# Modulation in four quarters on four column tiles, with four projections taken between them

## The reference, cut to what matters

```python
mod = jax.nn.silu(c) @ w_mod[layer] + b_mod[layer]          # 1024 -> 6 * 1024
mod_c = jax.nn.silu(c_ctx) @ w_mod[layer] + b_mod[layer]
sh1, sc1, g1, sh2, sc2, g2 = jnp.split(mod[:, None, :], N_MOD, axis=-1)
h = modulate(rmsnorm(x, norm1_g[layer]), sh1, sc1)           # h * (1 + scale) + shift
hc = modulate(rmsnorm(ctx, norm1_g[layer]), sh1c, sc1c)
k_g_c = heads(hc @ wk_g, GLA_HEADS)
...
(q_na, k_na, v_na, q_g, k_g, v_g, og, z_lr, m_a, m_b) = jnp.split(h @ w_in[layer], IN_OFFSETS, axis=-1)
```

## Time and profile before

| what | value |
|---|---|
| median of 3 runs | 3015.01 us (3014.63 to 3015.28) |
| the profiled execution's own time | 3013.45 us |
| its span | 3011.7 us, 33763 instructions |
| mean granted TensorE clock | 0.977 of full speed |
| TensorE matmul busy | 2855.4 us, 95% |
| VectorE, ScalarE, GpSimd busy | 1306.2, 1210.9, 1218.6 us (43%, 40%, 40%) |
| HBM read, written | 267.76 MB, 7.34 MB |

### The profile page before, as it was taken

One profiled execution on the slowest core, in us unless ns is written; L12 is line 12 of the kernel. 1 busy time (PEld: TensorE's weight loads), 2 busy tenths in 40 slices (PEclk: granted clock), 3 DMA queues, 4 the chain that ended last, 5 costly groups with the idle time before them and its releaser, 6 DMA issues.

```text
span 3011.7 us, 33763 instructions
## 1 busy us (share of the span) xinstructions
PE 2855.4 (95%) x13324; PEld 2238.1 (74%) x13324; DVE 1306.2 (43%) x1681; ACT 1210.9 (40%) x1753; POOL 1218.6 (40%) x555
## 2 busy tenths in 40 slices
PE   8997899899999999999998999979999999899997
PEld 4776677688888676677786888867766877778885
DVE  5656432441112667744415202268677353341123
ACT  4346663342223555443334222255545233442222
POOL 1122233344445463343444444436624434444442
PEclk9998999999999999999999999989999999999998
DMA  6333122232222311122231222222101223222221
GB/s 237 102 130 123 65 93 78 98 121 98 98 94 104 105 64 43 59 89 77 77 126 70 98 98 96 100 93 77 63 36 70 91 70 108 88 91 98 91 98 63
DMA packets 88989, 277.29 MB, mean 92 GB/s; under 512 B 10048, under 2 KB 10240, under 8 KB 88832
## 3 DMA queue, kind: packets, MB, share of 16 engines
q1 hardware_dynamic: 88832, 275.14, 25.7%
HBM read 267.76 MB, written 7.34 MB: 91 GB/s over the span
## 4 chain that ended last, share of the span: by engine, by line
PE 79%; DVE 12%; ACT 6%; issue 1%; DMA 1%; POOL 0%; SPq 0%; DVEq 0%; ACTq 0%; POOLq 0%
PE bank L1442 23%; PE bank L1444 23%; PE bank L1443 23%; PE bank L1678 2%; PE bank L1493 2%; PE bank L1628 1%; PE bank L1640 1%; DVE pageF L2395 1%; ACT L1723 1%; DVE pageF L2465 1%; DVE pageF L2469 1%; DVE pageR L2263 1%; PE bank L1669 1%; DVE pageF L1972 1%; DVE pageF L2198 1%
## 5 line engine op out<-in xcount | busy, mean ns | idle before, releaser
L2501 POOL TENSOR_TENSOR wlo<-wraw,whi 128x1024 fp32r<-128x1024 f32 x429 | 1047.4, 2444 | 1499.4 <-ACT whi L1706 1498.7
L1442 PE MATMUL bank<-pageR,whi 128*128 128x512 f32 x3552 | 1446.3, 407 | 65.0 <-ACT pageR L1865 27.4
L1444 PE MATMUL bank<-pageR,wlo 128*128 128x512 f32 x3552 | 1384.5, 390 | 0.0
L1443 PE MATMUL bank<-pageR,whi 128*128 128x512 f32 x3552 | 1384.3, 390 | 0.0
L1442 PEld LDWEIGHTS bank<-pageR,whi 128*128 128x128 f32 x3552 | 675.8, 190 | 247.5 <-issue 98.0
L1443 PEld LDWEIGHTS bank<-pageR,whi 128*128 128x128 f32 x3552 | 676.7, 191 | 153.6 <-issue 25.0
L1444 PEld LDWEIGHTS bank<-pageR,wlo 128*128 128x128 f32 x3552 | 675.1, 190 | 140.5
L1706 ACT ACTIVATE whi<-wraw 128x1024 fp32r<-128x1024 f32 x429 | 450.9, 1053 | 401.6 <-PE bank L1444 392.7
L1746 ACT ACTIVATE pageR<-pageF 128x512 fp32r<-128x512 f32 x136 | 85.9, 632 | 460.5 <-DVE pageF L2257 207.9
L2395 DVE SCALAR_TENSOR_TENSOR pageF<-pageF,prm 128x497 f32<-128x497 f32 (+9 forms) x180 | 202.3, 1124 | 2.7
L1827 ACT ACTIVATE pageF<-bank,smal 128x512 f32<-128x512 f32 x96 | 66.0, 687 | 148.8 <-DVE smal L2163 148.6
(11 more groups left out here) (200 smaller groups left out, 2119.8 us busy)
## 6 DMA issues: line engine op xcount, KB each, us to landing
wraw<-in_wst SPq DMA_DIRECT2D x429, 512.0 KB, 3.5
pageF<-in_wmod SPq DMA_DIRECT2D x96, 256.0 KB, 4.9
pageF<-in_xT SPq DMA_DIRECT2D x16, 256.0 KB, 4.3
pageF<-in_bias SPq DMA_DIRECT2D x16, 256.0 KB, 4.1
kept<-pageF SPq DMA_DIRECT2D x16, 256.0 KB, 4.7
pageF<-kept SPq DMA_DIRECT2D x16, 256.0 KB, 4.2
out_x<-pageF SPq DMA_DIRECT2D x8, 256.0 KB, 2.0
pageF<-in_cT SPq DMA_DIRECT2D x4, 256.0 KB, 9.3
```

What stands on the lines that cost most here:

```text
L1442: e.matmul(o, hi, xh, start=first, stop=False)
L1443: e.matmul(o, hi, xl, start=False, stop=False)
L1444: i = e.matmul(o, lo, xh, start=False, stop=last)
L2501: e.tensor_tensor(wlo[:, b % NH, :, :], wraw[:, b % NR, :, :], bc(whi[:, b % NH, :, :]), ALU.subtract).then_inc(*wlod.up(("wlo", b)))
```

## The change

The modulation's first 2048 columns are laid out in four quarters of 512: quarter q holds the shift and the scale of input tiles 2q and 2q+1, 128 columns each. `mod_mm` multiplies each 128 columns on a column tile of its own, with c padded to 32 stationary columns (c, c_ctx, 30 zeros), so that four results stand below each other in 128 partitions by 128 columns; one copy and one transpose turn a quarter. `planned` writes the steps in another order: the loads begin with c and x, the sum of squares takes every squared x tile in a product of its own (no additions on VectorE, no warm-up), Ln and Exp of x and of the context share their table loads, `h_in` is taken apart in four steps, and four projections (wq_g 0, w_lr, wk_g 0, wv_g 0) run k outermost, with the quarters 1 to 3 and the input tiles they give between their products. Their context parts lie in side banks. `w_next` may put a split every four tiles until it is 3 blocks ahead.

```diff
@@ w_next
-        if s % 8 == 0:
-            self.w_split(s // 8 + NH - 1)
+        if s % 4 == 0 and s >= 16 and self.split < s // 8 + NH:
+            self.w_split(self.split)
@@ planned, loads
-    step("load_fixed", "prm")
-    step("load_fixed", "ccol")
-    step("load_fixed", "cst")
+    step("load_fixed", "ccol")
     for k in range(8):
         pages.take(("X", k))
         step("load_x", k)
...
+        if k == 3:
+            step("load_fixed", "cst")
     for k in range(4):
         pages.take(("XC", k))
         step("load_ctx", k)
+    step("load_fixed", "prm")
+    for q in range(4):
+        if q < 3:
+            p.w_load(q)
         for k in range(8):
-            mod_load(8 * c + k)
+            mod_load(8 * q + k)
@@ planned, start
+    step("first_sums")
...
+    p.w_split(0)
+    step("load_fixed", "wal")
+    step("load_fixed", "tabG")
+    step("first_norms")
+    mod_rows(0)
+    step("first_newton", "x", T)
+    mod_columns(0)
+    h_in(0)
+    step("first_newton", "ctx", TC)
...
+    h_lo(0)
+    hc_in(0)
+    inputs(1)
     p.w_split(1)
+
+    def first_products():
+
+        items = [("wq_g", 0, False), ("w_lr", 0, True), ("wk_g", 0, True), ("wv_g", 0, True)]
+        for name, m, ctx in items:
+            mb.take(("o", name, m))
+            if ctx:
+                sbk.take(("oc", name, m))
+        rows, turned = {(0, 2): 1, (1, 3): 2, (3, 1): 3}, {(1, 0): 1, (2, 1): 2, (3, 3): 3}
+        for k in range(8):
+            for i, (name, m, ctx) in enumerate(items):
+                if (k, i) in rows:
+                    mod_rows(rows[k, i])
+                if (k, i) in turned:
+                    q = turned[k, i]
+                    mod_columns(q)
+                    inputs(2 * q)
+                    inputs(2 * q + 1)
...
+                s = p.w_next((name, m, k))
+                groups = [(("o", name, m), H[k])] + [(("oc", name, m), HC[k])] * ctx
+                step("mm", s, tuple(groups), k == 0, k == 7)
+                yield
@@ main_gla
-        yield from p.wide([("w_lr", 0), ("wk_g", 0)], H, HC)
+        yield from first_products()
@@ tensor
-                    e.matmul(o, csil[:, k, :], F(("wmod", 8 * c + k)), start=k == 0, stop=k == 7).then_inc(
-                        *dot.up(("modm", c, k), ("modb", c)))
+                    x = F(("wmod", 8 * q + k))
+                    w.wait_ge(*when("wmod", 8 * q + k))
+                    for t in range(4):
+                        i = e.matmul(o[32 * t:32 * t + 32, 0:128], csil[:, k, :], x[:, 128 * t:128 * t + 128],
+                                     start=k == 0, stop=k == 7)
+                    i.then_inc(*dot.up(("modm", q, k), ("modb", q)))
+
+            def first_sums():
                 w.wait_ge(*when("cst"))
...
+                for k in range(8):
+                    w.wait_ge(*when("q", "x", k))
+                    i = e.matmul(bank(("qm", "x")), ones, F(("q", "x", k)), start=k == 0, stop=k == 7)
+                i.then_inc(*dot.up(("qm", "x")))
...
+            def mod_columns(q):
+                clear(("modt", q))
                 w.wait_ge(*when("cst"))
...
+                w.wait_ge(*when("modrow", q))
+                e.transpose(bank(("modt", q))[:, 0:128], F(("modrow", q))[:, 0:128], ident).then_inc(
+                    *turn.up(("modt", q)))
@@ scalar
+            def first_norms():
+                norms = (("x", T), ("ctx", TC))
+                w.wait_ge(*when("prm"))
+                for t, width in norms:
+                    clear(("r", t))
+                    w.wait_ge(*when("qm", t))
+                    e.activation(F(("r", t))[:, 0:width], bank(("qm", t))[:, 0:width], ACT.Ln, scale=1.0 / 1024,
+                                 bias=col("eps")).then_inc(*fun.up(("rl", t)))
+                for t, width in norms:
+                    r = F(("r", t))[:, 0:width]
+                    w.wait_ge(*when("rl", t))
+                    e.activation(r, r, ACT.Exp, scale=-0.5).then_inc(*fun.up(("re", t)))
```

More of the change, by code:

```diff
@@ L342, in planned, with mod_rows @@
         step("load_ctx", k)
-    p.w_load(0)
-    for c in (1, 3):
+    step("load_fixed", "prm")
+    for q in range(4):
+        if q < 3:
+            p.w_load(q)
         for k in range(8):
[L346 to L349, removed]
+            mod_load(8 * q + k)
+    sbk.take(("qm", "x"))
+    sbk.take(("qm", "ctx"))
     step("silu_c")
-    sqx, sqc = Squares(p, "x"), Squares(p, "ctx", TC)
     for k in range(8):
[L354 to L358, removed]
-        for k in range(8):
[L360 to L385, removed]
+        pages.take(("q", "x", k))
+        step("x_square", k)
+    step("warm_ln")
+    for k in range(4):
+        pages.take(("q", "ctx", k))
+        step("ctx_square", k)
+    def mod_rows(q):
+        sbk.take(("modb", q))
+        step("mod_mm", q)
+        for k in range(8):
+            pages.give(("wmod", 8 * q + k), ("modm", q, k))
+        pages.take(("modrow", q))
+        step("mod_row", q)
+        sbk.give(("modb", q), ("modrow", q))
+    def mod_columns(q):
+        sbk.take(("modt", q))
+        step("mod_columns", q)
+        pages.give(("modrow", q), ("modt", q))
+        sbk.give(("modt", q), ("A1", q))
     H, HC = [("H", k) for k in range(8)], [("HC", k) for k in range(8)]
     def h_in(k):
-        for name in (("ht", k), ("H", k, "hi"), ("H", k, "lo"), ("hct", k), ("HC", k)):
+        for name in (("ht", k), ("H", k, "hi"), ("H", k, "lo")):
             pages.take(name)
@@ L392, in h_in, with h_lo, hc_in, hc_lo @@
         pages.give(("X", k), ("hs", k), ("q", "x", k))
+    def h_lo(k):
+        step("h_lo", k)
         pages.give(("ht", k), ("H", k, "hi"), ("H", k, "lo"))
+    def hc_in(k):
+        for name in (("hct", k), ("HC", k)):
+            pages.take(name)
+        step("hc_in", k)
+        if k % 2:
+            pages.give(("XC", k // 2), ("hcs", k), ("q", "ctx", k // 2))
+    def hc_lo(k):
+        step("hc_lo", k)
         pages.give(("hct", k), ("HC", k, "hi"), ("HC", k, "lo"))
-    for k in range(4):
+    def inputs(k):
@@ L397, in planned @@
         h_in(k)
-    mod_rows(1)
-    p.w_split(1)
[L400 to L409, removed]
+        hc_lo(k - 1)
+        h_lo(k)
+        hc_in(k)
+    step("first_sums")
+    for t, n in (("x", 8), ("ctx", 4)):
+        for k in range(n):
+            pages.give(("q", t, k), ("qm", t))
+        pages.take(("r", t))
+        pages.take(("rt", t))
@@ L476, in side_gla @@
             yield
+            yield from pause(0)
             for dr in range(2):
@@ L1460, in warm_up @@
-            def warm_up():
-                w.wait_ge(*when("cst"))
-                for i in range(6):
-                    t = e.matmul(bank(("warm",)), ident, cst[:, 0:4, :], start=True, stop=True)
-                t.then_inc(*dot.up(("warm",)))
-            def mod_columns(c, half_, part):
-                o, rw = bank(("modt", c)), F(("modrow", c))
-                clear(("modt", c))
+                    x = F(("wmod", 8 * q + k))
[3 more added lines that the diff above has]
+                                     start=k == 0, stop=k == 7)
@@ L1714, in warm_ln @@
             def warm_ln():
-                e.activation(smal[:, 255:256], col("one"), ACT.Ln).then_inc(*fun.up())
+                w.wait_ge(*when("cst"))
+                e.activation(smal[:, 255:256], ones[:, 0:1], ACT.Ln).then_inc(*fun.up())
             def rstd_act(t, width, scale):
@@ L1941, in scalar @@
             mine = {f.__name__: f for f in (
[L1942 removed]
+                silu_c, w_split, square, warm_ln, rstd_act, x_square, first_norms, mod_row, h_in, hc_in, halves, evict, evict_half, evict_turned, evict_z,
                 to_tokens, gla_gate, gla_gate_ctx, gla_scan, gla_decays, gla_out, soft_exp, na_out, silu_gate, tanh_gate, h2_hi,
```

155 lines of the change are left out of this document (101 added, 54 removed).

## The result

The changed kernel takes 2991.3 us (median of 4 runs, 2989.5 to 2992.8) against 3015.2 for the one before (3014.6 to 3015.8, 4 runs): ratio 0.9921, 95% interval 0.9903 to 0.9938. It is 23.9 us faster. The span of the profiled execution is 2987.7 us against 3011.7.

A forecast was written before the change was run, and what follows sets the result against it. TensorE was taken to bound the kernel, losing the first 49.2 us in which it has no projection to run. A gain of 12.4 us from the profiled 3013.45, with 1.56 added back, gave 3002.6 us, range 2993 to 3014.

The forecast's parts named there:

- Landing, sums, norm, 27.6: Start of the kernel: loads, sums of squares and norm let the first projection start at 27.6 us, not 49.23.
- A quarter's product, 2.9 us: Modulation on TensorE: a quarter's 32 products at 0.085 us each take 2.9 us, between bounds of 1.7 and 6.8.
- Mode changes: Changes of tiling mode around a quarter's block on TensorE: 0.2 us per block.
- Four projections, end 70.8: First four projections, with three quarters, transposes, mode changes and low clock between: done at 70.8 us.
- low clock: TensorE's clock at 0.50 after its idle time from 23.3 to 27.6: taken to cost 2.2 us.
- The wait at 87.71 goes: TensorE's 5.17 us wait in wv_g 1 goes, with 2.4 us of low clock; wv_g 1 ends at 80.7, gain 17.1.
- What is late next: VectorE delays vgc 0's transposes (1.7 us) and wv_g 2's ctx part (2.3 and 0.8), starting at 104.2; gain 12.4 us.
- "Behind that ... I take nothing, and 6 us either way": Side work 4 to 8 weight tiles later among the projections: no gain taken, 6 us (a sixth) either way.
- Rival 1: Shorter quarters, small new waits or shrinking later ones gain 6 us more, 2996; chance 0.17.
- Rivals 3 and 4: Column tiles run in turn, 3017, chance 0.08; clock stays at 0.50 until the four projections are done, 3034, chance 0.05.
- Rival 2: Side work sets the pace: waits from 130 to 560 us grow by a sixth, 3009; chance 0.20.

The follow-up runs named there:

- a_one_column: The changed kernel with its column tiles taken back, so a quarter's 32 products run one behind the other: 3009.2 us.
- a_side_earlier: The changed kernel with two pauses fewer in the GLA side work, so side steps stand where they stood in the kernel before: 3008.1 us.
- b_later_pre4: The kernel before, start untouched, with GLA side work 4 weight tiles later and w_mod loads 4 steps ahead: 2992.0 us.
- a_pre4: The changed kernel with the w_mod tiles loaded 4 steps ahead of their use instead of 2: 2980.3 us.
- a_pre4_decays_fill: The changed kernel with w_mod loads 4 steps ahead, pair 0's decays later and four unread identity products in TensorE's idle time: 2979.4 us.

## Why the prediction was right and wrong

- *Landing, sums, norm, 27.6*: right to 0.4 us at every mark (8.1, 17.6, 19.3, 22.3, 24.0 and 27.6 were 8.0, 18.0, 19.7, 22.5, 24.3 and 27.5). The chain through landing, norm and VectorE was the right one.
- *A quarter's product, 2.9 us*: too dear. The middle value from four row-and-column tiles was not the nearest row; per product it took 0.06 us, near the lower bound of 0.053. Three blocks gave back 2.9 us. Mode changes cost what was taken: 0.2 us for both ends of a block.
- *Four projections, end 70.8*: 69.1, by those 2.9 us and 0.8 less of low clock, and against them two waits for ScalarE's copies, 1.27 at 52.48 and 0.42 at 42.86, each behind a weight split. The low clock cost 1.4 (taken: 2.2). The forecast's model for it read the earlier trace rows a little short: at 0.50 or 1.00, a mean of 0.81 over 92 to 94 puts the rise at 92.8 and not at 92.4, so 5.1 us after the restart and not 4.7.
- *The wait at 87.71 goes*: yes, but another, of 4.88 us, took its place at 86.03. ScalarE's copies of vg 1 and vgc 1 stood behind a decay that waited 4.52 us for VectorE's scan. The forecast looked at the banks that these transposes need and not at the queue of the engine that copies.
- *What is late next*: 106.34 and not 104.2, for that reason. TensorE hardly waits for VectorE there: 0.89 us at 80.71 (taken: 1.7) and 0.32 at 106.34 (taken: 2.3 and 0.8 for the clock). In sum 11.8 us of gain at tile 128, for a forecast of 12.4. That the sum fits so well is partly luck: quarters, clock and these waits were taken too dear, and the 4.88 us that stood in no term made up for it.
- *"Behind that ... I take nothing, and 6 us either way"*: **this step failed.** It was 12.5 us, twice its bound. The step held that the same instructions 4 tiles later would cost about the same. Instead, two side chains that meet on ScalarE and VectorE moved against each other. Between tiles 128 and 400 TensorE's idle time fell from 31.3 to 21.0 us, with the clock behind it, and the shift alone, in the kernel before, gave 13.1 us in that stretch. The idle time stood in the earlier trace rows; that it could change by a sixth at most came from no row. A look into any of the four large waits would have shown what it hangs on, and that a shift could halve it or not. The scan over distances says more: 2 tiles to either side it was 13 to 18 us worse (with the loads ahead), so the sign of this term could hardly have been read off; going by those runs, a range of some 15 us to either side would have been fair.
- Rival 1 (more is gained) names this term among others, with 6 us. Rivals 3 and 4 are refuted: a_one_column shows what column tiles in turn would have cost (18 us), and the clock had risen by 31 us. Rival 2 is true in part, in a_side_earlier: side work set at its old distance takes 8 of the start's 12 us in the trace, some 4 by the medians.
- The forecast also carried what the start gains to the end one for one. With the shift that holds, 11.8 us at tile 128 and 12.4 between b_later_pre4 and a_pre4 at tile 400. Without it (a_side_earlier) a part is lost, whose size is open.

## What to carry to other kernels

When a change shortens one engine's start, ask what the other engines' chains gain; what they don't gain can be given back in part, as in a_side_earlier, unless the work is moved apart. A shift of side work against the main line is a change of its own: take the largest waits downstream and follow each back through the queues before costing it at nothing, and try the neighbouring distances on the chip, since a wait is as long as what happens to stand ahead of it in an in-order queue. And look at how long an idle engine waits for loads issued a fixed number of steps ahead: two numbers there gave 9 to 11 us by the medians, where this large rewrite gave 24.

## What the runs showed of the hardware

- Four column tiles of 32 stationary columns, float32, 128 moving columns each: 32 products in 1.95 us at full clock against 7.17 in one column tile, a factor of 3.7. The Trainium skill (TensorEngine Tiling (Array Packing), Theoretical Speedup) allows up to 4 there, and the trace agrees more closely than the forecast did.
- The granted clock was 0.50 in the changed kernel from 24 to 28 us, where TensorE had no work from 23.0 to 27.5, and 0.64 from 28 to 32. In a_pre4_decays_fill, where products whose result nobody reads fill most of that time, it was 1.00 in both. That was worth 2.3 us against a_pre4.
- An inverse root costs ScalarE two table loads, 1.28 us each, one ahead of Ln and one ahead of Exp, and the next instruction starts 0.02 us behind a load. The Trainium skill (ScalarE: Activation LUTs, What ACT_TABLE_LOAD costs) gives 1.28 us for the load and 1.38 for a drain; here the trace shows no second part. By its rule on sets (Table sets: the hidden batching unit), Ln and Exp could share one load; in these traces each pair has two.
